# Two SBUF addresses in a three-block forward pass: the low weight parts 64 bytes up, the arena 128 bytes up

## The reference

```python
def swiglu_ffn(h, w_in, w_out):              # 1024 -> 2 x 2816 -> 1024, eight of them
    gate, up = jnp.split(h @ w_in, 2, axis=-1)
    return (jax.nn.silu(gate) * up) @ w_out
...
    rkv = jnp.einsum('nbsc,cnd->nbsd', x3, w_rkv.reshape(C, 3, C))
...
    q = (h @ wq).reshape(B, S, XATTN_HEADS, XATTN_HEAD_DIM)
...
    z = jax.nn.gelu(h @ w_uv)                # 1024 -> 4096
```

## Time and profile before

| | |
|---|---|
| timed runs | 2577.43 and 2579.57 us, median 2578.5 us |
| profiled execution | 2573.3 us |
| its span, first to last instruction | 2571.5 us |
| TensorE matmuls | 2499.3 us busy, 97% of the span, 23,347 |
| TensorE weight loads | 2432.0 us busy, 95%, 23,347 |
| VectorE | 1745.9 us busy, 68% |
| ScalarE | 1317.2 us busy, 51% |
| GpSimd | 79.1 us busy, 3% |
| mean granted TensorE clock | 0.995 of full speed |

### The profile page before, as it was taken

The page is one execution under the profiler, slowest core; times in us unless marked ns, Lnnn a source line. Parts: engine busy times, 40 slices in busy tenths (PEclk is TensorE's granted clock), DMA queues, the critical chain, the costliest instruction groups (busy, mean ns, idle before and its releaser), DMA issues.

```text
span 2571.5 us, 60615 instructions
## 1 busy us (share of the span) xinstructions
PE 2499.3 (97%) x23347; PEld 2432.0 (95%) x23347; DVE 1745.9 (68%) x2868; ACT 1317.2 (51%) x1997; POOL 79.1 (3%) x122
## 2 busy tenths in 40 slices
PE   8998999999999999999999999899999999999999
PEld 8997877989999999989999999899999999999999
DVE  6757686667757667766756757967666566666774
ACT  5534544455545455555545547465455455555552
POOL 0000452000000000000000000000000000000000
PEclk9999999999999999999999999999999999999999
DMA  5663201535655664545654655245655565553564
GB/s 202 217 216 117 100 11 44 169 127 180 213 176 191 210 214 157 164 140 186 211 165 159 213 167 197 67 132 196 208 169 194 196 179 154 163 157 107 193 210 137
DMA packets 119825, 424.89 MB, mean 165 GB/s; under 512 B 16673, under 2 KB 24564, under 8 KB 119412
## 3 DMA queue, kind: packets, MB, share of 16 engines
q1 hardware_dynamic: 111616, 411.65, 48.4%
q10 hardware_dynamic: 8052, 11.04, 2.3%
HBM read 421.51 MB, written 1.12 MB: 164 GB/s over the span
## 4 chain that ended last, share of the span: by engine, by line
PE 85%; DVE 5%; ACT 2%; issue 2%; POOL 1%; DMA 0%; ACTq 0%; DVEq 0%; POOLq 0%
PE bank L478 19%; PE bank L472 19%; PE bank L477 19%; PE bank L398 5%; PE bank L400 4%; PE bank L399 4%; PE bank L2359 1%; ACT hi L341 1%; DVE lo L349 1%; PE bank L453 1%; PE bank L1761 1%; PE bank L454 1%; PE bank L455 1%; PE bank L1734 1%; PE bank L1280 1%
## 5 line engine op out<-in xcount | busy, mean ns | idle before, releaser
L349 DVE TENSOR_TENSOR lo<-raw,hi 128x1024 fp32r<-128x1024 f32 (+1 forms) x728 | 934.9, 1292 | 382.1 <-ACT hi L341 380.1
L341 ACT ACTIVATE hi<-raw 128x1024 fp32r<-128x1024 f32 (+1 forms) x728 | 782.7, 1106 | 302.8 <-PE bank L400 167.1
L472 PE MATMUL bank<-Hh,hi 128*128 128x256 f32 x3024 | 837.9, 277 | 3.3 <-DVE lo L349 2.0
L478 PE MATMUL bank<-Hh,lo 128*128 128x256 f32 x3024 | 838.5, 277 | 0.0
L477 PE MATMUL bank<-Hl,hi 128*128 128x256 f32 x3011 | 833.7, 277 | 0.0
L472 PEld LDWEIGHTS bank<-Hh,hi 128*128 128x128 f32 x3024 | 567.8, 188 | 4.5 <-DVE lo L349 4.3
L478 PEld LDWEIGHTS bank<-Hh,lo 128*128 128x128 f32 x3024 | 569.4, 188 | 0.0
L477 PEld LDWEIGHTS bank<-Hl,hi 128*128 128x128 f32 x3011 | 565.7, 188 | 0.0
L472 PE MATMUL bank<-Ah,hi 128*128 128x256 f32 x1408 | 389.8, 277 | 2.7 <-DVE lo L349 1.6
L478 PE MATMUL bank<-Ah,lo 128*128 128x256 f32 x1408 | 390.3, 277 | 0.0
L477 PE MATMUL bank<-Al,hi 128*128 128x256 f32 x1400 | 387.4, 277 | 0.0
(11 more groups left out here) (428 smaller groups left out, 4036.9 us busy)
## 6 DMA issues: line engine op xcount, KB each, us to landing
raw<-in_w SPq DMA_DIRECT2D x600, 512.0 KB, 3.4
raw<-in_w SPq DMA_DIRECT2D x128, 704.0 KB, 4.6
dB<-dil_bias ACTq DMA_DIRECT2D x16, 384.0 KB, 10.5
X<-in_x SPq DMA_DIRECT2D x2, 512.0 KB, 5.6
mem_x<-in_mem ACTq DMA_DIRECT2D x2, 512.0 KB, 3.3
gWS<-in_ws ACTq DMA_DIRECT2D x1, 1024.0 KB
gBS<-in_bs ACTq DMA_DIRECT2D x1, 1024.0 KB
out_x<-X SPq DMA_DIRECT2D x4, 256.0 KB, 2.6
```

The costliest lines, as they stand in the source:

```text
L341: act.activation(k.hi[:, q, :w], k.raw[:, q, :w], ACT.Copy).then_inc(k.hi_ready, 1)
L349: dve.tensor_tensor(k.lo[:, q, :w], k.raw[:, q, :w], k.hi[:, q, :w].bitcast(F32), ALU.subtract).then_inc(k.lo_ready, 1)
L472: pe.matmul(out, wh, xh, start=first, stop=False)
L478: mm = pe.matmul(out, wl, xh, start=False, stop=last)
```

## The change

A tensor `skew` of 16 floats (64 bytes a partition) that nothing reads or writes is declared between `hi` and `lo`. The arena's base is computed by another formula.

```diff
         self.raw = sb("raw", [P, RING, WIDE * P])
         self.hi = sb("hi", [P, RING, WIDE * P], F32R)
+        self.skew = sb("skew", [P, P // 8])
         self.lo = sb("lo", [P, RING, WIDE * P], F32R)
         self.X = sb("X", [P, NC, T])
...
         self.sel = sb("sel", [P, NC * 16])
-        self.base = -(-nc.sbuf_base // 64) * 64
+        self.base = -(-nc.sbuf_base // P) * P + P // 2
         self.room = nc.sbuf_usable_end - self.base
```

## The result

The changed kernel takes 2634.8 us (median of 2 runs, 2632.4 and 2637.1) against 2578.5 us: slower, ratio 1.023, 95% interval 1.021 to 1.025. The forecast was 2577 us, practically no change, with a range of 2540 to 2630; the result lies 4.8 us above the range.

What follows compares the result with a forecast made beforehand. The prediction took TensorE's matmul stream as the bound. With all terms at zero it stayed between the profiled execution's 2573.3 us and the timed median of 2578.5 us, at 2577 us, range 2540 to 2630 us.

Steps and rivals of the forecast that it cites:

- The pace as the place where an address can act: TensorE's stream of split matmuls: steady paces of 113.3 or 117.6 ns, the one thing an address could act on.
- VectorE's and the transfers' terms: Up to 15 us of VectorE's `lo` instruction, hidden behind TensorE, and 0.6 us of X's load; transfers taken at zero.
- the slower rival: New offset makes the slower matmul pace win: +22 us (2592 to 2625 us, 0.14) or +66 us (2625 to 2650 us, 0.11).
- every window near 850: Sign of slower matmuls: about 850 in each 100 us trace window, instead of 883 to 887 in some.
- Two stable paces existed with one and the same relation of addresses, so the address alone is not what chooses between them.: Reason for pricing the 6208 loads from `lo` at zero, between a gain of 16 us and a loss of 22 us.
- the `lo` third: Third matmul of each triple, weights from `lo`, 6208 loads: gain 16 us or lose 22 us, taken zero.
- the other two thirds: Matmuls with weights from `hi`; if triples lock as a whole, from 47 us gained to 66 us lost, taken zero.
- every one at the slower: Upper end: all 18,624 split matmuls at the slower pace, 66 us lost.
- the third-only version: Only matmuls loading from `lo` settle at 117.7 ns: +22 us, 2600 us; chance 0.14 for 2592 to 2625 us.
- L1280 with 0 apart shows no slowing: Plain fp32 matmuls of 128 columns, weights and moving operand both in the arena, 111.6 ns each; argument against slowing.
- the estimate of 91 us: All 18,624 matmuls at 109.2 ns instead of 114.1: 91 us less, 3.5%; no trace row showed that pace.

Runs made afterwards that it cites:

- `lo` alone: Kernel before with `lo` (and X and the small buffers) 64 bytes up, `hi` and arena at their old places modulo 256: 2636.5 us, ratio 1.023.
- `Al` alone: Kernel before with the moving operand `Al` (and `RKV` behind it) 64 bytes up, nothing else moved: 2596.3 us, ratio 1.007.

## Why the prediction was wrong

*The pace as the place where an address can act* was right, and so was the way to read it. In all fifteen runs the time roughly follows the count of matmuls in the full windows, and in the changed kernel VectorE's and the transfers' terms, taken at zero, were near it (1224 ns for 1222; 6.0 us of waiting for X instead of 5.8). The sign named for the slower rival, "every window near 850", is what came.

*"Two stable paces existed with one and the same relation of addresses, so the address alone is not what chooses between them."* This is the step that failed. It is true that the address does not choose between the two; it decides whether the fast one exists. At 192 the stream has both (885 and 852 matmuls in 100 us). At 64 no such window has more than 851, at 0 none has more than 835. On this step rested both zeros, for the `lo` third and for the other two thirds; together they measured 64 us of span. Two paces at one address were evidence that the stream is sensitive to timing, and I read them as evidence that addresses do not matter.

*The distances were worked out modulo 128.* The prediction mentions modulo 256 and prices it at nothing. By modulo 128 the arena's move is empty; measured alone it costs 2627.5 - 2575.1 = 52 us, where the whole change costs 56. The two halves do not add up: `lo` alone costs 61.5 us.

*The other two thirds: "taken zero, with both ends kept".* The upper end there was "every one at the slower", 66 us more. That is what happened in size: 64 us of span. The rival that forecast it gave 2645 us and a chance of 0.11; the measured one lies between it and the third-only version (2600 us). Its mechanism was half right: moving one buffer does cost more than that buffer's third (`lo` alone, 61.5 us where all loads at 128 cost 71), but the changed stream does not settle at the steady slower pace; it runs through unequal steps with a mean close to it. That the two means lie so close is not explained by its mechanism.

*"L1280 with 0 apart shows no slowing"* was the argument against that rival, and it misled: at distance 0 the split products were at their slowest, 120.0 ns. Those rows are of another kind of product, with 128 columns, and did not carry over to this one.

*The range.* The term that should have widened it was known: 66 us for all loads, for which the trace had some 1500 matmuls of one feed-forward block as a witness. With two places of the layout moving at once and a good timing that was known to be only one of two, 0.11 was too little.

What stays open is why. The runs show that the pace goes by a distance with a period of 256 bytes, that a move of either side can spoil it, and that a mixture of 192 and 128 costs more than its share (61.5 us, not 24). The mixtures of 64 with 192 and of 0 with 192 cost 41 and 56 us, near their shares of 35 and 60. They do not show what in the chip repeats every 256 bytes, nor whether a load meets its own matmul or the one before it. The page "SBUF — State Buffer" of the Trainium skill, section "Who interferes with whom", gives TensorE two independent read ports and lets it wait for no other engine. No run here tests the second part. As to the first, the time of a load and a matmul side by side goes by the distance of their addresses, 113.3 to 120.0 ns; the page says nothing of that, and the measurement decides. The 109.2 ns that the prediction took from "TensorE: Matmul & The Clock Gate" of the Trainium skill, section "Back-to-back issue gap", were not reached in any full window; 113.3 was the least. That section gives its formula for a matmul by itself, and for streams of loads and matmuls it has 81 ns at 128 columns and 131 ns at 512, with no figure for 256; so the estimate of 91 us in the prediction stood on a figure for another case.

## What to carry to other kernels

Where TensorE is the bound and each matmul has a weight load of its own, count matmuls in full windows of the trace: if equal pairs show two paces, the pace hangs on timing, and the distance between the weight buffer and the moving operand modulo 256 bytes is worth a scan, since it is free. The only layouts here that kept the time of before had every buffer at the one good distance, so fix the bases by formula; here the good place came about by the sum of the small buffers' sizes. In this kernel a shift of 64 bytes between weights and moving operands cost from 0.7% (`Al` alone) to 2.3% (`lo` alone), and 3.6% with both weight buffers up and the arena moved. A shift of everything together cost nothing. No kernel run here beats the layout of before beyond the noise. Whether 192 is the good distance for another kernel was not tried.

## What the runs showed of the hardware that was not expected

A load of 128 columns and a matmul of 256 `fp32r` columns that run side by side take, per pair, by distance: 113.3 or 117.7 ns at 192, 116.6 at 32 (117.9 in one block), 117.6 at 64, 117.3 or 118.7 at 160, 118.3 at 224, 118.6 at 128, 120.0 at 0. The granted clock was 1.00 in all these windows; of the windows shown it was lower only in the changed kernel's at 1390 us (0.99). The fast timing at 192 comes and goes at restarts of the stream; once there, it lasts for a thousand matmuls and more. The same feed-forward block, with the same distances, had 852 matmuls in 100 us in one kernel and 882 in another (256 bytes up). The 4.4 ns between the two timings over one such block are 7 us, and may be a source of the scatter between executions of one and the same kernel (2564 to 2585 us for the kernel before over the four sets of runs), which is my reading and was not tested.
